# Second norm of a decoder trunk: sums of squares taken as rows of tokens instead of columns

## The reference, cut to what matters

```python
def rmsnorm(x, g):
    y = x * rsqrt(mean(x * x, axis=-1) + EPS)
    return y * g

def merge_and_ffn(x, a, b, ...):
    h = sigmoid(ga) * (a @ w_oa) + sigmoid(gb) * (b @ w_ob)
    x = x + h @ w_out
    xn = rmsnorm(x, ln2_g)                              # the second norm
    return x + square(relu(xn @ w_up)) @ w_down
```

## Time and profile before

| what | value |
|---|---|
| runs | 1530.99, 1531.38, 1531.77 us; median 1531.38 |
| profiled execution | 1531.51 us |
| its span | 1529.8 us, 1.7 us less |
| mean granted clock of TensorE | 0.999 |
| PE busy | 1513.4 us, 99% |
| DVE, ACT, POOL busy | 1074.9, 764.1, 192.2 us |

### The profile page before, as it was taken

The page is one execution under the profiler, slowest core; times in us unless marked ns, Lnnn a source line. Parts: engine busy times, 40 slices in busy tenths (PEclk is TensorE's granted clock), DMA queues, the critical chain, the costliest instruction groups (busy, mean ns, idle before and its releaser), DMA issues.

```text
span 1529.8 us, 28796 instructions
## 1 busy us (share of the span) xinstructions
PE 1513.4 (99%) x12186; PEld 1484.4 (97%) x12186; DVE 1074.9 (70%) x1445; ACT 764.1 (50%) x1153; POOL 192.2 (13%) x196
## 2 busy tenths in 40 slices
PE   8999999999999999999999999999999999999998
PEld 7988989999999999999999999999999999999997
DVE  7666564316686786857698777867797769776975
ACT  6565565325546745555434755334543454345533
POOL 7132232200000410000010200000000000000001
PEclk9999999999999999999999999999999999999999
DMA  9611011318694354545697466364545545454512
GB/s 251 207 58 30 29 30 31 97 44 215 208 304 135 91 112 135 139 114 142 171 214 218 106 132 176 101 165 104 152 105 154 122 138 138 135 135 116 153 29 111
DMA packets 109495, 200.65 MB, mean 131 GB/s; under 512 B 19696, under 2 KB 47344, under 8 KB 102040
## 3 DMA queue, kind: packets, MB, share of 16 engines
q1 hardware_dynamic: 92008, 128.74, 25.5%
q0 software_dynamic: 9840, 62.94, 21.4%
q10 hardware_dynamic: 7520, 7.14, 1.5%
HBM read 121.81 MB, written 19.30 MB: 92 GB/s over the span
## 4 chain that ended last, share of the span: by engine, by line
PE 96%; DVE 2%; issue 1%; ACT 0%; DMA 0%; POOL 0%; SPq 0%; DVEq 0%
PE ps L1780 73%; PE ps L1536 14%; PE ps L1524 3%; PE ps L1622 2%; PE ps L1604 2%; PE ps L1562 1%; PE ps L1758 1%; DVE y_t L1513 1%; DMA x_stage<-in_x_prompt 0%; DVE xp_lo L1282 0%; DVE k_lo L1135 0%; POOL prob L634 0%; PE ps L1544 0%; DVE prob L1159 0%; DVE xg L1100 0%
## 5 line engine op out<-in xcount | busy, mean ns | idle before, releaser
L1780 PE MATMUL ps<-xp_lo,wp_hi 128*128 128x258 f32 x3136 | 889.1, 284 | 0.0
L1780 PE MATMUL ps<-xp_hi,wp_hi 128*128 128x258 f32 x3136 | 886.2, 283 | 1.3 <-DVE xp_lo L1282 0.7
L1780 PE MATMUL ps<-xp_hi,wp_lo 128*128 128x258 f32 x3136 | 882.9, 282 | 0.0
L1780 PEld LDWEIGHTS ps<-xp_hi,wp_hi 128*128 128x128 f32 x3136 | 593.8, 189 | 2.2 <-DVE xp_lo L1282 1.0
L1780 PEld LDWEIGHTS ps<-xp_hi,wp_lo 128*128 128x128 f32 x3136 | 593.5, 189 | 0.0
L1780 PEld LDWEIGHTS ps<-xp_lo,wp_hi 128*128 128x128 f32 x3136 | 591.3, 189 | 0.0
L776 ACT ACTIVATE wp_hi<-wbuf 128x1024 fp32r<-128x1024 f32 x196 | 207.8, 1060 | 529.3 <-PE ps L1780 529.1
L1276 DVE TENSOR_TENSOR wp_lo<-wbuf,wp_hi 128x1024 fp32r<-128x1024 f32 x196 | 246.4, 1257 | 156.4 <-ACT wp_hi L776 156.4
L1536 PE MATMUL ps<-xn_hi,w_hi 128*128 128x344 f32 x456 | 150.6, 330 | 0.0
L1536 PE MATMUL ps<-xn_hi,w_lo 128*128 128x344 f32 x456 | 145.7, 320 | 0.0
L1536 PE MATMUL ps<-xn_lo,w_hi 128*128 128x344 f32 x456 | 145.7, 320 | 0.0
(11 more groups left out here) (209 smaller groups left out, 1565.4 us busy)
## 6 DMA issues: line engine op xcount, KB each, us to landing
wbuf<-wbuf POOLq DMA_DIRECT2D x57, 1024.0 KB, 7.5
wbuf<-in_w_up SPq DMA_DIRECT2D x24, 1024.0 KB, 5.3
wbuf<-in_w_down SPq DMA_DIRECT2D x24, 1024.0 KB, 5.3
wbuf<-in_w_in SPq DMA_DIRECT2D x18, 1024.0 KB, 5.7
raw<-in_w_in SPq DMA_DIRECT2D x38, 256.0 KB, 3.3
wbuf<-in_w_ob SPq DMA_DIRECT2D x6, 1024.0 KB, 7.6
wbuf<-in_w_oa SPq DMA_DIRECT2D x6, 1024.0 KB, 5.1
wbuf<-in_w_out SPq DMA_DIRECT2D x6, 1024.0 KB, 9.1
```

Source lines behind the costliest of these rows:

```text
L1780: last = mm(ps[:, 2 * p + b, 0:HN], w[:, (2 * n + p // 2) % 2, k, p % 2 * P:(p % 2 + 1) * P], x[n % 2][:, k, b * HN:(b + 1) * HN], start=( ...
```

## The change

The sums of squares now come out as rows. In `sums`, `ones[:, 0:32]` is the weight (32 columns of the array) and `sq_acc` moves through, 258 tokens each time; four such matmuls write partitions 0 to 31, 32 to 63, 64 to 95 and 96 to 127 of the bank, where each of the 32 partitions of a group holds the same row of 258 sums. The variance and the power work on that tile of 128x258 (`rs_row`), and the store takes one partition out of each group, a row of 1032 bytes, four times. `rs_row` lies in row 5 of the region, over `sq_acc[:, 1, 0:516]`, and ACT waits at i = 2 for the four stores instead of for `sq_summed`.

```diff
+        rs_row = place("rs_row", [P, 2, T // 4], F32, r_1 + 4 * (KT // 2 + 1) * T)
...
                         sp.wait_ge(rs_ready, 1)
-                        with nc.allow_non_contiguous_dma(reason="one number of each token, 4 KB"):
-                            sp.dma_start(rs_keep[0, 0:SEQ].rearrange("(t p) -> p t", p=P), rstd[:, 0:NBLK]).then_inc(rs_kept, 16)
-                            sp.dma_start(rs_keep[0, SEQ:T].rearrange("(p a) -> p a", a=1), rstd[0:NB, NBLK:NTOK]).then_inc(rs_kept, 16)
-                        sp.wait_ge(rs_kept, 32)
+                        for c in range(4):
+                            sp.dma_start(rs_keep[0:1, c * HN:(c + 1) * HN], rs_row[32 * c:32 * c + 1, 1, :]).then_inc(rs_kept, 16)
+                        sp.wait_ge(rs_kept, 4 * 16)
                         sp.dma_start(rstd_b[:, :], rs_keep.to_broadcast([P, T])).then_inc(rb_in, 16)
...
                     pool.wait_ge(var_ready, 1)
-                    nc.gpsimd.tensor_tensor(rstd[:, :], var[:, :], mhalf[:, :], ALU.pow).then_inc(rs_ready, 1)
+                    nc.gpsimd.tensor_tensor(rs_row[:, 1, :], rs_row[:, 0, :], mhalf[:, 0:1].to_broadcast([P, HN]), ALU.pow).then_inc(rs_ready, 1)
...
                     elif g == G_UP and i == 2:
-                        act.wait_ge(sq_summed, 4)
+                        act.wait_ge(rs_kept, 4 * 16)
...
-                ts(var[:, 0:NBLK], ps[:, bank, 0:NBLK], 1.0 / D, EPS, ALU.mult, ALU.add)
-                return ts(var[0:NB, NBLK:], ps[0:NB, bank, NBLK:NTOK], 1.0 / D, EPS, ALU.mult, ALU.add)
+                return ts(rs_row[:, 0, :], ps[:, bank, 0:HN], 1.0 / D, EPS, ALU.mult, ALU.add)
...
-                for t in range(NTOK):
-                    last = mm(ps[0:ROWS[t], bank, t:t + 1], sq_acc[:, 0, toks(t)], ones[:, 0:1], start=True, stop=True)
+                for c in range(4):
+                    last = mm(ps[32 * c:32 * c + 32, bank, 0:HN], ones[:, 0:32], sq_acc[:, 0, c * HN:(c + 1) * HN],
+                              start=True, stop=True)
```

## The result

The changed kernel takes 1564.8 us (median of 5 runs, 1564.14 to 1565.28), the kernel before 1531.38 us. The ratio is 1.0217, with a 95% interval of 1.0205 to 1.0228: slower by 33.4 us. The forecast was 1568 us in a range of 1559 to 1575. The profiled execution took 1565.28 us, its span is 1563.5 us, 33.7 us longer than the one before.

What follows compares the result with a forecast made beforehand. TensorE, busy 99% of the span, bounds the kernel, so its waits count in full: 1531.5 + 35.4 (stop behind the power and stores) + 1.5 (clock) = 1568.4 us, forecast 1568, range 1559 to 1575.

Steps and rivals of the forecast that it cites:

- The power: On POOL, 128x258: price goes with elements in a partition, 0.159 us each, so 41.4 us (39.9 by the smaller slope).
- Rivals 1 and 2: POOL's power has a flat price, 1530.3 us, 6 in 100; or half the price an element, 1548 us, 5 in 100.
- VectorE: Variances become one 128x258 instruction from PSUM, 0.42 us, running from 886.25 to 886.67.
- The sums: On TensorE, 32-column matmuls run side by side: 0.7 us instead of 1.90 us.
- The stores: Four row stores land 8.5 us behind rs_ready, beside POOL's addition; the other bound, with nothing beside, is 4.5 us.
- rival 3: The power's line holds and the stores land undisturbed in 4.5 us: 1564.4 us, 1563 without the clock; 25 in 100.
- The stop of TensorE: In product i = 3, TensorE waits for activations 3.29 us behind rs_kept, until 939.94 instead of 904.55: 35.4 us lost.
- The limit: rs_kept (stores landed) may come as late as 901.26 us without making TensorE wait in product i = 3.
- rival 1: POOL's power has a flat price for long rows, 1.2 us, so no wait appears: 1530.3 us; 6 in 100.
- The clock: TensorE's clock falls to its lower level in the gap; cost between 0 and 2.9 us, taken as 1.5 us.
- (a): Spreading load, late with rs_kept, delays VectorE and ACT for i = 4: 12.7 us against 14.8, covered by 2 us.
- (b): Weight load and POOL's addition for i = 5: about 21 us, then 2.3, needed at 25.6; covered by 2 to 5.

Runs made afterwards that it cites:

- e_half: Changed kernel, but POOL raises only 129 of the 258 columns to the power and copies the others; 1544.23 us.
- e_64: Changed kernel, but POOL raises only 64 of the 258 columns to the power and copies the other 194; 1533.15 us.
- e_apart: Kernel before, but POOL issues its addition add_s4(G_UP) only when the two stores of rstd have landed; 1530.88 us.
- e_own: Changed kernel with rs_row over rstd_b, so ACT at i = 2 waits for sq_summed, no longer for the stores; 1562.15 us.
- e_behind: Kernel before, plus two 128x129 powers into a spare tile on POOL, behind rs_ready and ahead of add_s4(G_UP); 1555.20 us.
- e_mult: Changed kernel, but POOL multiplies the 128x258 tile by -0.5 instead of raising it to the power; 1529.55 us.
- e_sqrt: Changed kernel, but VectorE's reciprocal and ScalarE's square root replace POOL's power; rs_row over rstd_b, ACT waits for sq_summed; 1529.96 us.

## Why the prediction was right, step by step

**The power**, on which all rested: 41.4 us forecast, 41.54 measured. Extrapolating from 9 elements to 258 along a line that three small sizes gave came true, and e_half and e_64 put two more points on it. (The lower bound was misreckoned: with the smaller slope of 0.154 it is 40.1 us, not 39.9.) Rivals 1 and 2 fall with POOL's row of 41.54 us itself. The Trainium skill, "GPSIMD Engine Reference", section 3.1, has a tensor_tensor of POOL at about 2.6 cycles an element, an estimate of 0.56 us here. The same instruction as a product took 0.61 us, which agrees; the power does not follow it.

**VectorE**: 886.67 forecast for the end of the variances, 886.18 + 0.42 = 886.60 measured.

**The sums**: 0.7 us forecast, 0.57 until the next product (885.05 - 884.48). Side by side, as the attention's row of 32-column matmuls had it.

**The stores**: this term was mis-sized. 8.5 us were taken, by the two stores of before, because POOL's addition stood beside both; 4.36 were measured, next to the other bound of 4.5. e_apart shows the fault of the choice: the row that was nearest in its company (the addition) was far off in kind (1032 pieces of 4 bytes). The number is that of rival 3, 1564.4 us, given a quarter of the chance, and lies 0.4 us from the median; its reason, that the rows would land undisturbed, isn't what happened, since the addition ran beside them. This term makes the forecast 4.1 us too long; 0.9 us come back from the clock and from where product i = 3 starts.

**The stop of TensorE**: the chain from `rs_kept` to the matmul at k = 2 was put at 3.29 us and took 935.98 - 932.61 = 3.37. With the stores as measured the sum gives 928.15 + 4.4 + 3.3 - 904.55 = 31.3 us; 31.6 were lost. The difference is mostly the 904.55: it was counted from ACT's start at 903.83, but TensorE began product i = 3 at 903.63, so the matmul at k = 2 stood at 904.35.

**The limit** of 901.26 us for `rs_kept` was put too late, by these 0.2 us and by the 1.2 us of the shorter sums, which bring TensorE to the wait earlier. e_64 shows it: its stores had landed at 901.20, and TensorE had a gap of 1.71 us. That shrinks the room in which rival 1 would have ended without a wait, and leaves the forecast as it is, since its loss was counted from the kernel before.

**The clock**: 1.5 us taken between 0 and 2.9, 2.2 measured.

**What is late next**: (a) and (b) were said to be covered once TensorE has been stopped, and there is one gap and no second one besides the microsecond at 935. e_own shows what (a) costs if it stands first, 31 us; e_behind does so for POOL's part of (b), 24 us with powers of 45 us. The prediction called their cover independent of the power's time, which holds in the changed kernel only because all of it starts at one and the same moment.

**The gain** of 1.2 us by shorter sums was there and was lost in the same wait, as said; e_mult makes it visible at 1.3 us against the faster runs of before. The prediction missed that the old sums also cost a fall of the clock in some executions.

## What to carry to other kernels

Before an operation is moved to another layout, multiply by the number of elements in a partition, not of results: 1032 numbers as 128 x 9 took 1.8 us of POOL's power, as rows in 32 copies 41.5. Take the price of an element from the trace for just this operation, since the power was 68 times as dear as the product of the same shape, and look for two sizes of it that give the slope. And when one late thing holds up several, removing the wait that the chain names gives back only the distance to the next.

## What the runs showed of the hardware that was not expected

- A power on POOL costs 0.16 us an element of a partition, a product of 128x258 takes 0.61 us in all.
- TensorE's clock fell from 2.4 to 1.2 GHz without a gap, behind 1.9 us of one-column matmuls (the trace of e_apart), at a cost of 1.5 us; and behind a gap of only 1.7 us (the trace of e_64). By the groups of times the first happened in 11 of 27 runs, the second in 6 of 11. Behind the same sums as 32-column matmuls of 258 tokens (0.6 us) the traces of e_mult and e_sqrt have no such fall, and their 22 times have no second group.
- After 31 us of idleness the lower clock lasted 7.3 us from the first matmul (933.32 to 940.66), 4.7 of them steady work.
- Stores of 1032 separate 4-byte pieces land 8.5 to 9.4 us after the first issue, four rows of 1032 bytes 2.8 to 4.4 us.
- VectorE's reciprocal of 258 elements takes 1.77 us, where a tensor_scalar of the same size out of PSUM takes 0.42.
